# First norm of a transformer kernel: its weight row loaded once and spread by TensorE, its identity loaded alone, and the second pair of row transposes moved inside the first half chunk

## What is computed

```python
def rmsnorm(x, g):
    xf = x.astype(jnp.float32)
    y = xf * lax.rsqrt(jnp.mean(xf * xf, axis=-1, keepdims=True) + EPS)
    return (y * g.astype(jnp.float32)).astype(x.dtype)
...
        h = rmsnorm(x, norm_mix_pre[l])
        proj = jnp.einsum('bsd,de->bse', h, w_in[l])
```

## Time and profile before

| what | value |
|---|---|
| median of three runs | 3244.49 us |
| profiled execution | 3247.14 us |
| its span | 3245.4 us |
| PE busy | 3152.0 us, 97% of the span |
| DVE busy | 1691.0 us, 52% |
| ACT busy | 1191.9 us, 37% |
| share of PE in the chain that ended last | 88% |
| PE busy in the first 300 us | 277.84 us |

### The profile page before, as it was taken

The page is one execution under the profiler, slowest core; times in us unless marked ns, Lnnn a source line. Parts: engine busy times, 40 slices in busy tenths (PEclk is TensorE's granted clock), DMA queues, the critical chain, the costliest instruction groups (busy, mean ns, idle before and its releaser), DMA issues.

```text
span 3245.4 us, 42276 instructions
## 1 busy us (share of the span) xinstructions
PE 3152.0 (97%) x17113; PEld 2604.4 (80%) x17113; DVE 1691.0 (52%) x2230; ACT 1191.9 (37%) x1612; POOL 145.5 (4%) x203
## 2 busy tenths in 40 slices
PE   8999999999999999999999899999999999999999
PEld 7768888888876788888887488888878888788887
DVE  3574456553456535555447755552553443555543
ACT  3562234443345422444232344332331222344332
POOL 2030000000103000000002200000000000000000
PEclk9999999999999999999999999999999999999999
DMA  6203323232412222332232123322322121222222
GB/s 173 63 27 104 96 89 113 90 97 98 117 50 65 73 97 94 101 103 90 91 104 66 40 85 104 100 95 94 102 65 83 61 91 60 71 93 95 95 88 89
DMA packets 229781, 285.02 MB, mean 88 GB/s; under 512 B 5156, under 2 KB 188492, under 8 KB 229388
## 3 DMA queue, kind: packets, MB, share of 16 engines
q1 hardware_dynamic: 225628, 266.89, 25.3%
q0 software_dynamic: 4016, 16.16, 2.1%
HBM read 280.93 MB, written 2.10 MB: 87 GB/s over the span
## 4 chain that ended last, share of the span: by engine, by line
PE 88%; DVE 8%; ACT 2%; issue 1%; POOL 0%; DMA 0%; DVEq 0%; ACTq 0%; POOLq 0%
PE ps L1581 19%; PE ps L1582 19%; PE ps L1583 19%; PE ps L1694 6%; PE ps L1696 6%; PE ps L1695 6%; DVE t_wlo L1040 2%; ACT t_whi L674 1%; PE ps L1620 1%; PE ps L1618 1%; PE ps L1619 1%; DVE t_vb L1500 1%; PE ps L1787 1%; PE ps L2153 1%; PE ps L1823 1%
## 5 line engine op out<-in xcount | busy, mean ns | idle before, releaser
L1040 DVE TENSOR_TENSOR t_wlo<-t_wraw,t_whi 128x2048 fp32r<-128x2048 f32 x252 | 583.3, 2315 | 1321.2 <-ACT t_whi L674 1321.2
L1581 PE MATMUL ps<-t_hh,t_whi 128*128 128x512 f32 (+1 forms) x2704 | 1013.1, 375 | 13.6 <-DVE t_accv L1229 5.1
L1582 PE MATMUL ps<-t_hl,t_whi 128*128 128x512 f32 (+1 forms) x2704 | 1002.9, 371 | 0.0
L1583 PE MATMUL ps<-t_hh,t_wlo 128*128 128x512 f32 (+1 forms) x2704 | 1002.9, 371 | 0.0
L674 ACT ACTIVATE t_whi<-t_wraw 128x2048 fp32r<-128x2048 f32 x252 | 482.8, 1916 | 1374.2 <-PE ps L1583 953.8
L1581 PEld LDWEIGHTS ps<-t_hh,t_whi 128*128 128x128 f32 x2704 | 511.1, 189 | 117.2 <-issue 15.3
L1582 PEld LDWEIGHTS ps<-t_hl,t_whi 128*128 128x128 f32 x2704 | 511.3, 189 | 87.8 <-issue 2.4
L1583 PEld LDWEIGHTS ps<-t_hh,t_wlo 128*128 128x128 f32 x2704 | 510.9, 189 | 87.6
L1694 PE MATMUL ps<-t_whi,t_midh 128*128 128x512 f32 x704 | 274.4, 390 | 0.0
L1696 PE MATMUL ps<-t_whi,t_midl 128*128 128x512 f32 x704 | 274.0, 389 | 0.0
L1695 PE MATMUL ps<-t_wlo,t_midh 128*128 128x512 f32 x704 | 273.9, 389 | 0.0
(11 more groups left out here) (275 smaller groups left out, 3704.4 us busy)
## 6 DMA issues: line engine op xcount, KB each, us to landing
t_wraw<-in_w_in_dram SPq DMA_DIRECT2D x46, 1024.0 KB, 5.3
t_wraw<-in_w_up_dram SPq DMA_DIRECT2D x44, 1024.0 KB, 5.1
t_wraw<-in_ffn_w_in_dram SPq DMA_DIRECT2D x44, 1024.0 KB, 5.1
t_wraw<-in_w_kv_dram SPq DMA_DIRECT2D x24, 1024.0 KB, 5.1
t_wraw<-in_w_down_dram SPq DMA_DIRECT2D x20, 1024.0 KB, 5.0
t_wraw<-in_ffn_w_out_dram SPq DMA_DIRECT2D x20, 1024.0 KB, 5.0
t_wraw<-in_w_branch_dram SPq DMA_DIRECT2D x12, 1024.0 KB, 5.0
t_wraw<-in_w_q_dram SPq DMA_DIRECT2D x12, 1024.0 KB, 5.1
```

The lines of the kernel that those rows point to most:

```text
L1040: v.tensor_tensor(wlo[slot][:, :], wraw[slot][:, :], whi[slot][:, :].bitcast(F32), ALU.subtract).then_inc(w_lo, 1)
L1581: te.matmul(out, wh, xh, start=first, stop=False)
L1582: te.matmul(out, wh, xl, start=False, stop=False)
L1583: return te.matmul(out, wl, xh, start=False, stop=last)
```

## The change

Four things change.

1. POOL no longer loads the norm's weights into all partitions. It loads the identity alone (64 KB), then the weights as one row of 4 KB into partition 0 (`first_gain`), then waits until x row 3 has landed and loads the other 256 KB of `base`. `base_in` stands for that last part alone and is waited for where PE transposes the parameter rows and where ACT makes `rotg`.
2. DVE sets a row of 128 ones. PE multiplies it with the row of weights: two products of contraction 1 and 512 columns into PSUM banks 2 and 3, so that each partition holds all weights. DVE's `scale_row` of the first norm reads them from there.
3. In the order of PE, rows 2 and 3 are transposed after the first `row_half` of chunk 0, not before it.
4. In ACT's code the roots of rows 2 and 3 stand at the end of the first turn of the loop, not at the start of the second. The instructions come out in the same order as before.

```diff
         post_gain, pre_gain = gain[:, 0:D], gain[:, D:2 * D]
+        first_gain, ones = gain[0:1, D:2 * D], gain[0:1, 0:P]
+
+        def gain_banks():
+
+            return bank(2, 2)
...
-            spread_row(pre_gain, PRE[0])
-            pool.dma_start(base[:, :], A["c_base"]).then_inc(base_in, 16)
+            pool.dma_start(ident, A["c_base"][:, 0:P]).then_inc(ident_in, 16)
+            pool.dma_start(first_gain, PRE[0].rearrange("(o d) -> o d", o=1)).then_inc(gains_in, 16)
+            pool.wait_ge(x_in[3], 16)
+            pool.dma_start(base[:, P:5 * P], A["c_base"][:, P:5 * P]).then_inc(base_in, 16)
...
             for c in range(2):
-                pre_root("pre0", 2 * c)
-                pre_root("pre0", 2 * c + 1)
+                if c == 0:
+                    pre_root("pre0", 0)
+                    pre_root("pre0", 1)
                 row_hi("pre0", hh, 2 * c)
                 row_hi("pre0", hh, 2 * c + 1)
                 act.wait_ge(w_loaded[c], 16)
                 sc.activation(whi[c][:, :], wraw[c][:, :], ACT.Copy).then_inc(w_hi, 1)
+                if c == 0:
+                    pre_root("pre0", 2)
+                    pre_root("pre0", 3)
...
                 c = FIRST[f"a_qkv{l}"]
+                act.wait_ge(base_in, 16)
...
                     p = int(name[3:])
-                    if p == 0:
-                        dve.wait_ge(gains_in, GAIN["pre0"])
                     dve.wait_ge(pre_rooted, 4 * p + b + 1)
                     ch.link(v.reciprocal(pre_r[b], pre_rms[b]))
                     g = pre_gain
+                    if p == 0:
+                        dve.wait_ge(gain_spread, 1)
+                        g = gain_banks()
...
+            v.memset(ones, 1.0).then_inc(ones_set, 1)
             v.memset(small[:, 16:17], 0.0).then_inc(drained, 2)
...
                 turn_row("pre0", 0)
                 turn_row("pre0", 1)
+                pe.wait_ge(w_lo, 1)
+                pe.wait_ge(h_lo, SPLIT["pre0"] + 4)
+                row_half(0, (hh, hl), 0, 0, bank(0))
+                pe.wait_ge(rows_ready, ROW_OF["pre0"] + 4)
                 turn_row("pre0", 2)
                 turn_row("pre0", 3)
-                pe.wait_ge(w_lo, 1)
-                pe.wait_ge(h_lo, SPLIT["pre0"] + 4)
-                rows_half(0, (hh, hl), 0, 0)
+                row_half(0, (hh, hl), 0, 1, bank(4))
                 pe.wait_ge(h_lo, SPLIT["pre0"] + 8)
                 rows_half(0, (hh, hl), 1, 0).then_inc(w_used, 1)
...
-            pe.wait_ge(base_in, 16)
+            pe.wait_ge(ones_set, 1)
+            pe.wait_ge(gains_in, GAIN["pre0"])
+            for i in range(2):
+                ins = te.matmul(bank(2 + i), ones, first_gain[:, i * T:(i + 1) * T], start=True, stop=True)
+            ins.then_inc(gain_spread, 1)
+            pe.wait_ge(ident_in, 16)
             for l in range(2):
...
                 if l == 0:
+                    pe.wait_ge(base_in, 16)
                     pe.wait_ge(init_in, 16 * len(param_loads))
```

More of the change, by code:

```diff
@@ L239, in build @@
         x_in = [sem(f"x_in{b}") for b in range(4)]
-        base_in = sem("base_in")
+        base_in, ident_in, ones_set, gain_spread = sem("base_in"), sem("ident_in"), sem("ones_set"), sem("gain_spread")
         init_in, init_turn, init_out, stored = sem("init_in"), sem("init_turn"), sem("init_out"), sem("stored")
```

## The result

The changed kernel took 3255.48 us in the median of 20 executions (3246.21 to 3258.04), the kernel before 3246.3 in the same set (3243.89 to 3247.62, 20). The ratio is 1.0025, with a 95% interval of 1.0019 to 1.0032: **9.2 us slower**, where the prediction had 2.5 us faster. The profiled execution took 3257.46 us, its span is 3255.7, that is 10.3 more than the span of before. The loss is made early. The first load of `w_branch`, a moment that both programs share, is issued at 179.31 us before and at 188.47 after, 9.2 later.

What follows compares the result with a forecast made beforehand. PE, busy 97% of the span, bounds the kernel; only its idle or slow time can be won. Row 0 0.07 us earlier plus reordering and clock gave 2.5 us: 3244.49 - 2.5 = 3242.0 us, range 3239.5 to 3245.5.

Steps and rivals of the forecast that it cites:

- Arrival of the weights: POOL's queue at the start: the 4 KB row is signalled at 5.9 us, bounds 3.7 and 9.0.
- Spreading: PE's two fp32 products of 512 columns at half clock take 2.1 us together, filling the banks at 8.0.
- Reading from PSUM at no cost: DVE's scaling of row 0 from PSUM costs 0 extra, upper bound 0.2 us.
- Memset, ACT's order, the rest of `base`: Extra memset, ACT's edit and the later 256 KB load in the front cost 0.
- Reordering: PE's front: chunk 0 starts at 17.9, not 19.40; with the clock, A comes 2.5 us earlier, span 1.7 to 3.1.
- A: End of chunk 1 on PE, at its parameter transposes: 46.98 us before, forecast 44.5.
- the case "6.0 us": Clock rises 6.0 us after PE's start: 24 products slow, 4 transposes slow, 12 fast; A at 45.3, 1.7 earlier.
- No wait for the low parts of rows 2 and 3: After the second transposes: low parts ready at 26.5 us, PE has products until 27.3, so no wait.
- Does it last?: Chunk 3: load at 49.1, drain done 54.8, PE needs it at 56.6; slack 1.8 us, so the gain stays.
- The row lands late: Front rival: row landing after 8.4 us loses the gain; at 9.0 3245.1, dear form 3248.7; chance 0.13, dear 0.04.
- Chunk 3 late: Rival: chunk 3's load after 50.9 us stops PE before it; at 53.4 nothing is left, 3244.5; chance 0.07.
- The clock rival: Front: PE's clock rises only after the transposes and the change does almost nothing, 3244.4; chance 0.05.

Runs made afterwards that it cites:

- `order_held`: Kernel before with PE's reordering alone and POOL's run of 32 subtractions held behind DVE's drains in both layers: 3238.08 us, ratio 0.9975.
- held kernel before: Kernel before with POOL's 32 subtractions in two halves, each held until DVE did a certain drain, in both layers: 3239.84 us, ratio 0.998.
- `order_only`: Kernel before with PE's new order and nothing else changed: 3247.56 us, ratio 1.0007.
- `front_only`: Changed kernel with PE's old order put back, all four rows transposed ahead of the first product: 3252.47 us, ratio 1.0019.
- `before_more`: Kernel before with 16 more POOL subtractions ahead of its run in layer 2: 3250.72 us, ratio 1.0017.
- `row_sp`: Changed kernel with POOL's run held in both layers, the 4 KB row moved to first load on SP's queue: 3237.06 us, ratio 0.9971.

## Why the prediction was wrong

- **Arrival of the weights, 5.9 us: wrong, 7.38.** The step took the moment at which POOL's queue began to move (4.8) and added bytes and 0.8 us. The row was the second load on that queue, and the identity, ahead of it, took 4.8 us from its issue, the row 5.4. My dear bound (9.0) held, the chosen value did not: +1.5 us.
- **Spreading, 2.1 us: wrong, 3.76.** The earlier trace rows say x22 for a line that I read as 22 products. Each fp32 product is two of these records, so two products are four: 4 by 0.88 is 3.5, the first one is longer. The step's arithmetic had the answer, with the wrong count: +1.65 us. The Trainium skill (FP8 and Floating Point Precision, section on TensorE's precision) gives four passes through the array for true fp32; from this, two products of 512 columns at 1.2 GHz would be 3.4 us, an estimate that the 3.76 bear out, and that I hadn't used.
- **Reading from PSUM at no cost: right.** DVE's scaling took 1.28 us from the two banks as from SBUF. The 0.06 us more that the prediction took from the Trainium skill (VectorE: DVE Perf Modes, section on the TRN2 errata) don't show.
- **Memset, ACT's order, the rest of `base`: right.** None of them is in the chain.
- **Reordering, 2.5 us with bounds of 1.7 and 3.1: right.** A came 1.67 us earlier with the order alone, at the low bound, and 2.4 in the new front (48.64 against 51.03). In the changed kernel all 24 products were slow and the transposes fast, which is the case "6.0 us" but for the first transposes. In `order_held` the clock rose at 21.2 us, 3.3 after PE's start, and A was 2.5 earlier than in the held kernel before (44.16, 46.68).
- **No wait for the low parts of rows 2 and 3: right.** The products that need them start at 31.36 us, the low parts were there at 30.47, and PE didn't stop.
- **"Does it last?": the step that failed, and with it the sign.** It asked only whether chunk 3's load is late, and took 5.7 us from ACT's start to DVE's drain from one place of the trace. The load itself kept to what it was tied to: the low parts of rows 2 and 3 ended at 30.47 us (forecast 26.5), and the load landed at 52.95 (forecast 49.1), both 4 us later. But from ACT's start to the last drain it took 13 us instead of 5.7, since POOL's run held DVE. That is 5.3 us of wait and 2.4 of clock, 7.7 of the 11.7 us between 2.5 faster, as forecast, and 9.2 slower; the other 4.1 stand at A already (48.64 against 44.5), most of them from the two terms of the front. The row that told it stood in the same trace: 8.14 us for the same line in layer 2, with PE waiting 6.0. The prediction took this line's price from one meeting that went well.
- **The rivals.** "The row lands late" was the nearest, with its 8.4 us as the point of decision: landed at 7.38 but spread at 11.27, it acts like a row that lands at 9.2. By the prediction's working that is +0.8 us; A moved by 1.66, and even so 7.5 of the 9.2 are missing. "Chunk 3 late" named the place and not the cause. Its decisive point (50.9) moves with A, which came 4.1 us later than forecast, to 55.0; the load at 52.95 kept it, and with POOL held and the load as late there was no stop. The clock rival is refuted: the clock rose with the transposes (0.50 until 26.5 us, 1.00 from 27.0, the transposes end at 28.39), not behind them. All three signs that the prediction named for being wrong came: the spread started behind 7 (7.51), A lies outside 43.9 to 45.3, and PE stops between chunk 2 and chunk 3.
- **The range** of 3239.5 to 3245.5, and 0.96 for "within 0.2%", knew nothing of an outcome that depends on which of two engines gets in first. The 20 executions of the changed kernel spread over 11.8 us, the three shown of before over 1.7.

## What to carry to other kernels

Read the longest instruction of a group as well as its mean: where the same VectorE operation takes 2.3 us here and 8 there, look at what GpSimd does at the time, and move or break GpSimd's run before touching anything else; here that was worth 6.2 us, more than the 2.5 forecast for the change. Ask of each edit that shifts a stage by some us which back-to-back run of another engine it now falls under. A tiny load that everything waits for is worth a place ahead of the big ones: here, first on SP's queue, it landed in 1.5 us instead of 5.4.

## What the hardware showed that I had not expected

- A back-to-back run of GpSimd subtractions (12.8 us, 32 by 0.40) kept a VectorE subtraction of two SBUF operands out for 5.2 to 10.8 us, over 13 to 27 instructions, in nine meetings of these profiles; in eight of them VectorE ended 2.15 us behind the run. In layer 0, VectorE got in within one instruction when it came 4.6 and 5.4 us into the run (before, `order_only`) and, in seven held kernels, 3.7 to 4.2 us into it; it stayed out at 4.7, 5.1 and 5.2 (`front_only`, `before_more`, changed kernel). What decides between them is open. A wait of GpSimd for itself after each 8 made 11 executions of 11 good.
- A 4 KB load on GpSimd's queue took 5.4 us while SP's queue read x and chunk 0, 4.6 when it stood first there, and 1.5 as the first load of SP's own.
- PE's clock rose 3.3, 5.6 and 5.3 us after the first product of chunk 0 in `order_held`, the changed kernel and `row_sp` (at 21.2, 26.9 and 21.8 us), with the same work. An earlier start in `row_sp` (16.52 against 17.86 us) was eaten that way: A gained 0.4 us out of 1.3.
